# The order of branch groups and mixing steps, and which weight chunks live in one-time places

## The chip, the cores and the metric

One core of one Trainium2 chip runs the whole kernel. The metric is device time in microseconds (us). TensorE is called PE, VectorE DVE, ScalarE ACT and SyncE SP, as in the profile.

## The reference, cut to what matters

One encoder layer on 256 tokens of width 1024, in float32:

```
h      = rmsnorm(x);  proj = h @ w_in + b_in            # q, k, v, xr, yr, gates
merged = g_attn * (attn @ w_attn_o) + g_rec * (rec @ w_lru_o)
x      = x + merged @ w_out
h      = rmsnorm(x);  logits = h @ w_router + b_router  # top 4 of 32 experts
gu     = xb @ w_gu[e] + b_gu[e]                         # per expert, 1024 -> 2048
act    = clamp(g) * sigmoid(1.702 g) * (clamp(u) + 1)
y     += gate * (act @ w_down[e] + b_down[e])           # 1024 -> 1024
out    = rmsnorm(x + y)
```

The 32 experts hold 32 x 12.6 MB = 403 MB of weights, read once each from HBM.

## The kernel before

**Two halves.** The first half computes the token mixer. Its weights come as 15 "pre" chunks, each 128 x 4096 float32 (2 MB), that are split into a high and a low part; a product is three matmul passes over the parts. The second half walks the experts in order, 64 gathered tokens at a time; a step (one expert) uses six chunks of 2 MB, four of gate and up weights (`gate_up`, j = 0 to 3) and two of down weights of the expert before (`down`, j = 4 and 5). Step 0 has no down part, so expert chunks are numbered k = 0 to 3 for step 0 and then six to a step. PE uses the chunks in the order of k.

**Places.** Expert chunks live in a ring of eight 2 MB places: slots 0 to 6 (6 is `LOWS`) and slot 7, the tile `wide`. `SLOT_ORDER` says in which order the ring is walked. Two more chunks, named in `EXTRA`, go once into memory that the first half no longer needs: `late` takes the first, `pbuf` and `xr_flat` the two halves of the second. These one-time places are not refilled. `RING_CHUNKS` lists the chunks that use the ring; the one at index i goes to place `SLOT_ORDER[i % 8]` and its load waits until the chunk at index i - 8 has been used (`chunk_used`).

**Who issues.** SP issues all loads in one program order, each behind its wait. The first loads into a ring place wait for the first half to let go of it (`FREED`): slots 4 and 5 for six branch groups, slots 0 and 1 for `mixed_ps` 1 (mixing steps 0 to 3 done), `LOWS` for all eight branch groups, slots 2 and 3 for `mixed_ps` 2 (all mixing done). Half of `EXTRA[1]` and half of the chunk for `wide` are loaded some 30 us earlier, as memory allows. SP's program is written out for the first steps; a loop takes over after that.

**The work around the change.** `branches(g)`, g = 0 to 7, is one group of 128 output columns of the two branch products on PE (36 matmuls in two halves of a PSUM bank); banks 4 and 5 alternate. For g of 2 and more it first waits for `merged_ok` g - 1, which is the merge of group g - 2, the last user of its bank. On DVE the loop over g waits for the group (`branch_ps`), merges it with the gates in five instructions (L847, L849, L851, and the high and low parts, L621 and L624) and raises `merged_ok`; between groups it makes the low parts of pre chunks 12, 13 and 14 (`split_low`, L624). `mix(c)`, c = 0 to 3, multiplies merged block c with the first half of `w_out` into banks 0 to 3 (12 matmuls); `mix_end(n)` does blocks 4 to 7. Behind it come the second norm, the router and the first gather, and then step 0 of the experts.

Of the kernel before, what the change touches and what calls it, by code (L numbers as in the profile page):

```python
# [23 lines left out]
KD = D // P  # L24
# [15 lines left out]
SLOTS = 8  # L40
PAIRS = 3
PRE = 15
PER = 6
UNROLL = 4
# [11 lines left out]
def encoder_layer(nc, x, consts, squares, rows, pre, w_lru, w_gu, w_down, b_down, out):  # L56
# [5 lines left out]
    with ctx:  # L62
# [16 lines left out]
        LOWS = 2 * PAIRS  # L79
# [139 lines left out]
        dn_chunk = w_down.rearrange("e (p j r) n -> e j p (r n)", j=2, r=4)  # L219


        SLOT_ORDER = [4, 5, 0, 1, LOWS, SLOTS - 1, 2, 3]
        EARLIER = [5, 0, 5, 0, 4, 0, 1, 1]
        FREED = {4: [(branch_ps, 6)], 0: [(mixed_ps, 1)], LOWS: [(branch_ps, KD)], 2: [(mixed_ps, 2)]}

        EXTRA = (6, 11)
        RING_CHUNKS = [k for k in range(PER * UNROLL) if k not in EXTRA]

        def chunk_no(n, j):

# [41 lines left out]
        def expert_src(e, j):  # L272
            c = gu_chunk[e, j] if j < 4 else dn_chunk[e, j - 4]
            return c if isinstance(e, int) else c.rearrange("o p n -> (o p) n")


        @block.sync
        def _(sp):
            for t in range(T):
                sp.dma_start(x_sb[:, t, :], x[t * P:(t + 1) * P, :]).then_inc(x_in, 16)  # L280
            def expert_load(k):

                n, j = step_of(k)
                i = RING_CHUNKS.index(k)
                s = SLOT_ORDER[i % SLOTS]
                if i >= SLOTS:
                    n0, j0 = step_of(RING_CHUNKS[i - SLOTS])
                    sp.wait_ge(chunk_used[j0], n0 + 1 if j0 < 4 else n0 + AHEAD)
                else:
                    for freed in FREED.get(s, ()):  # L290
                        sp.wait_ge(*freed)
                sp.dma_start(slot(s), expert_src(n if j < 4 else n - 1, j)).then_inc(slot_full[s], 16)

            def half_load(dst, k, r, full):
                n, j = step_of(k)
                sp.dma_start(dst, expert_src(n, j)[:, r * 2048:(r + 1) * 2048]).then_inc(full, 16)

            for c in range(PRE):
                if c == 13:
                    sp.wait_ge(group_done, 32)  # L300
                    sp.wait_ge(gate_ps, 32)
                elif c == 14:
                    sp.wait_ge(pv_ps, NQ)
                    half_load(extra_rows(1, 0), EXTRA[1], 0, extra_full[1])
                    half_load(wide[:, 0:2048], 5, 0, slot_full[SLOTS - 1])
                    sp.wait_ge(branch_ps, 3)
                elif c >= PAIRS:
                    sp.wait_ge(*CONSUMED[c - PAIRS])
                sp.dma_start(whole(c), pre[c, :, 0:WIDTH[c]]).then_inc(slot_full[PLACE[c]], 16)
                if c == 1:  # L310
                    sp.dma_start(pbuf[:, 0:QKV + NH * HD], rows[0:1, 0:QKV + NH * HD].to_broadcast([P, QKV + NH * HD])
                                 ).then_inc(bias_in, 16)
                    o = QKV + NH * HD
                    sp.dma_start(brt[:, :], rows[0:1, o:o + NE].to_broadcast([P, NE])).then_inc(bias_in, 16)
                if c == 2:
                    sp.dma_start(cst[:, C_COS:], consts[:, C_COS:]).then_inc(tables_in, 16)
                    sp.dma_start(ring[LOWS][:, KD * TOK:], w_lru[0]).then_inc(lruw_in, 16)
                if c == 6:
                    sp.wait_ge(gate_ps, 16)
                    sp.dma_start(ring[LOWS][:, KD * TOK:], w_lru[1]).then_inc(lruw_in, 16)  # L320
            for k in range(5):
                expert_load(k)
            half_load(wide[:, 2048:], 5, 1, slot_full[SLOTS - 1])
            n, j = step_of(EXTRA[0])
            sp.dma_start(late[:, :], expert_src(n, j)).then_inc(extra_full[0], 16)
            sp.wait_ge(merged_ok, KD)
            half_load(extra_rows(1, 1), EXTRA[1], 1, extra_full[1])
            for k in RING_CHUNKS[6:-2]:
                expert_load(k)
            sp.wait_ge(passes_ok, 1)  # L330
            n_pass = sp.value_load(passes[0:1, 0:1], min_val=NE, max_val=NE * ROUNDS)

            def loop_load(n, i, place, j, e):
                s = SLOT_ORDER[(PER * i - 2 + place - len(EXTRA)) % SLOTS]
                n0, j0 = divmod(place - SLOTS, PER)
                sp.wait_ge(chunk_used[j0], sp.snap(n + (i + n0 + (1 if j0 < 4 else AHEAD))))
                src = expert_src(e, j) if isinstance(e, int) else expert_src(bass.ds(e, 1), j)
                sp.dma_start(slot(s), src).then_inc(slot_full[s], 16)

            with sp.Fori(UNROLL, n_pass, UNROLL) as n:  # L340
                for i in range(UNROLL):
                    e = sp.snap(sp.to_reg((n + i) & (NE - 1)), min_val=0, max_val=NE - 1)
                    e_before = sp.snap(sp.to_reg((n + i - 1) & (NE - 1)), min_val=0, max_val=NE - 1)
                    for j in range(PER):
                        loop_load(n, i, j, j, e if j < 4 else e_before)
            loop_load(n_pass, 0, 0, 4, NE - 1)
            sp.wait_ge(chunk_used[LAST_AFTER[1]], sp.snap(n_pass + LAST_AFTER[0]))
            for r in range(4):
                sp.dma_start(slot(LAST_SLOT)[:, r * D:(r + 1) * D],
                             expert_src(NE - 1, 5)[:, r * D:(r + 1) * D]).then_inc(last_in[r], 16)  # L350
            for n in range(2 * T):
                t, cols = n // 2, slice((n % 2) * BANK, (n % 2 + 1) * BANK)
                sp.wait_ge(fin_ok, n + 1)
                sp.dma_start(out[t * P:(t + 1) * P, cols], x_sb[:, t, cols]).then_inc(out_done_dma, 16)
            sp.wait_ge(out_done_dma, 16 * 2 * T)
# [224 lines left out]
        def _(dve):  # L580
# [263 lines left out]
            for g in range(KD):  # L844
                o = (g % 2) * TOK
                dve.wait_ge(branch_ps, g + 1)
                nc.vector.scalar_tensor_tensor(out=m_a[:, o:o + TOK], in0=gA[:, g, :], scalar=1.0,  # L847
                                               in1=half(4 + g % 2, 0), op0=ALU.add, op1=ALU.mult)
                link(nc.vector.scalar_tensor_tensor(out=m_r[:, o:o + TOK], in0=gR[:, g, :], scalar=1.0,  # L849
                                                    in1=half(4 + g % 2, 1), op0=ALU.add, op1=ALU.mult))  # L850
                link(nc.vector.tensor_tensor(merged[:, g, :], m_a[:, o:o + TOK], m_r[:, o:o + TOK], ALU.add))  # L851
                link(high_part(merged_hi[:, g, :], merged[:, g, :]))
                low_part(merged_lo[:, g, :], merged[:, g, :], merged_hi[:, g, :]).then_inc(merged_ok, 1)
                if g == 1:
                    split_low(12)
                if g == 2:
                    split_low(13)
                if g == 4:
                    split_low(14)

            dve.wait_ge(merged_ok, KD)
# [164 lines left out]
        def _(pe):  # L1026
# [149 lines left out]
            def branches(g):  # L1176
                first = 12 * g
                if g == 0:
                    pe.wait_ge(rec_split, 1)
                    pe.wait_ge(group_read, 32)  # L1180
                for i, c in enumerate(BR_CHUNK):
                    if first <= BLOCKS * i < first + 12:
                        chunk_in(c)
                if g >= 2:
                    pe.wait_ge(merged_ok, g - 1)
                w = [[b[:, q % BLOCKS, :] for b in w_br[q // BLOCKS]] for q in range(first, first + 12)]
                product(half(4 + g % 2, 1), [(w[k], (rec_hi[:, k, :], rec_lo[:, k, :])) for k in range(KD)])
                if g == 0:
                    pe.wait_ge(attn_split, 1)
                product(half(4 + g % 2, 0), [(w[KD + k], (attn_hi[:, k, :], attn_lo[:, k, :])) for k in range(4)]  # L1190
                        ).then_inc(branch_ps, 1)
# [8 lines left out]
            def mix(c):  # L1200
                if c == 0:
                    chunk_in(MIX_CHUNK[0])
                pe.wait_ge(merged_ok, c + 1)
                for n in range(2 * T):
                    ins = mix_bank(n, c)
                if c == 3:
                    ins.then_inc(mixed_ps, 1)
# [10 lines left out]
            for g in range(5):  # L1218
                branches(g)
            mix(0)  # L1220
            mix(1)
            branches(5)
            mix(2)
            mix(3)
            branches(6)
            branches(7)
            def second_transposes(t):
                pe.wait_ge(x2_ok, 2 * t + 2)
                if t == 1:
# [257 lines left out]
```

## Time and profile before

| | before |
|---|---|
| median of 3 runs | 1167.56 us (1165.97 to 1172.44) |
| profiled execution | 1171.78 us, of which span 1170.0 us |
| PE busy | 1086.2 us (93%) |
| DVE, ACT busy | 383.3 us (33%), 234.1 us (20%) |
| HBM read | 438.46 MB |
| mean granted TensorE clock | 0.993 |

The span runs from the first to the last instruction. The time of a run is a little longer than its span. Times inside the execution are counted from the start of the span. A busy PE is not PE at its peak, since matmuls overlap and their ends are modelled.

### The profile page before, as it was taken

Reading aid. Unit: us, or ns where it says so; the run is one execution under the profiler, and the core shown is the slowest. Engines: PE = TensorE matmul, PEld = TensorE weight load, DVE = VectorE, ACT = ScalarE, POOL = GpSimd, SP = SyncE. Lnnn points to the kernel's source line nnn. Section 1 sums busy time; section 2 is a strip of 40 time slices with the busy share of each in tenths; the row PEclk is TensorE's granted clock in tenths of the full one; section 3 lists DMA queues with packets and bytes.
Section 4 is the critical chain, followed back from the end, with each engine's and each line's share of the span. In section 5 each row is a group of like instructions: output and inputs, shape, how many; then the busy total and the mean of one; then the engine's idle time right before and its main releaser. Section 6 shows DMA issues by size and latency. Waiting matters only on the chain.

```text
span 1170.0 us, 13209 instructions
## 1 busy us (share of the span) xinstructions
PE 1086.2 (93%) x5391; PEld 507.2 (43%) x5391; DVE 383.3 (33%) x671; ACT 234.1 (20%) x371; POOL 0.2 (0%) x4
## 2 busy tenths in 40 slices
PE   6998999999999999999898989898989999999997
PEld 5997889833333333333233323332333333333332
DVE  6995699442322222221212121212121212212122
ACT  4387863111111111110101010101010101011112
POOL 0000000000000000000000000000000000000000
PEclk9998999999999999999999999999999999999999
DMA  8442326997999999999999999999999999999995
GB/s 342 179 182 96 121 89 272 390 428 308 401 430 425 429 427 428 428 427 429 429 429 427 429 429 429 429 427 429 427 429 429 429 427 430 427 429 430 428 429 239
DMA packets 32619, 439.90 MB, mean 376 GB/s; under 512 B 3760, under 2 KB 3888, under 8 KB 5712
## 3 DMA queue, kind: packets, MB, share of 16 engines
q1 hardware_dynamic: 32112, 438.53, 89.2%
q10 hardware_dynamic: 480, 0.99, 0.2%
q8 instruction: 20, 0.33, 0.1%
q14 instruction: 7, 0.06, 0.0%
HBM read 438.46 MB, written 1.05 MB: 376 GB/s over the span
## 4 chain that ended last, share of the span: by engine, by line
PE 59%; DMA 36%; DVE 2%; ACT 1%; issue 1%; SPq 0%; DVEq 0%
DMA slot<-in_w_gu_dram 29%; PE ps L1332 24%; PE ps L1034 12%; PE ps L1341 9%; DMA slot<-in_w_down_dram 6%; PE ps L1304 4%; PE ps L1285 3%; PE ps L1075 1%; PE ps L1089 1%; PE ps L1299 1%; PE ps L1386 1%; DMA slot<-in_pre_dram 1%; PE ps L1132 1%; PE ps L1263 1%; PE ps L1153 1%
## 5 line engine op out<-in xcount | busy, mean ns | idle before, releaser
L1332 PE MATMUL ps<-slot,lru 128*64 128x512 f32 x896 | 203.3, 596 | 25.7 <-DMA slot<-in_w_gu_dram 25.3
L1332 PE MATMUL ps<-slot,qT 128*64 128x512 f32 x880 | 200.2, 596 | 15.8 <-DMA slot<-in_w_gu_dram 14.2
L1341 PE MATMUL ps<-slot,lru 128*64 128x512 f32 x880 | 199.9, 596 | 15.3 <-DMA slot<-in_w_down_dram 14.9
L1332 PEld LDWEIGHTS ps<-slot,lru 128*64 128x64 f32 x896 | 63.0, 137 | 152.1 <-issue 113.1
L1332 PEld LDWEIGHTS ps<-slot,qT 128*64 128x64 f32 x880 | 62.6, 136 | 146.3 <-issue 131.8
L1341 PEld LDWEIGHTS ps<-slot,lru 128*64 128x64 f32 x880 | 61.1, 137 | 133.6 <-issue 114.3
L555 ACT ACTIVATE lru<-ps 128x512 f32<-128x512 f32 x32 | 19.1, 597 | 420.4 <-PE ps L1332 420.4
L990 DVE TENSOR_TENSOR lru<-ps,cst 128x1024 f32<-128x1024 f32 x32 | 39.2, 1225 | 142.9 <-PE ps L1386 142.9
L967 DVE TENSOR_SCALAR lru<-sq,x_sb,small 128x64 f32<-128x64 f32 x66 | 17.7, 311 | 189.4 <-PE ps L1285 189.4
L1034 PE MATMUL ps<-wide_r,slot_r 128*128 128x256 f32 x492 | 67.6, 290 | 0.0
L1034 PEld LDWEIGHTS ps<-wide_r,slot_r 128*128 128x128 f32 x492 | 62.9, 196 | 4.5 <-issue 4.4
L1304 PE MATMUL ps<-lru 128*128 128x512 f32 x136 | 63.9, 593 | 0.9 <-DVE lru L1014 0.9
L984 DVE COPY lru<-ps 128x512 f32<-128x512 f32 x32 | 22.1, 692 | 128.1 <-PE ps L1332 128.1
L1285 PE MATMUL ps<-hn,lru 128*64 128x512 f32 x264 | 62.9, 593 | 0.9 <-DVE lru L904 0.9
L624 DVE TENSOR_TENSOR slot_r<-slot,slot_r 128x4096 fp32r<-128x4096 f32 (+1 forms) x14 | 59.7, 4269 | 2.6 <-ACT slot_r L383 2.5
L557 ACT ACTIVATE lru<-lru 128x512 f32<-128x512 f32 x32 | 20.2, 630 | 199.7 <-DVE lru L994 199.7
L541 ACT ACTIVATE qT<-ps 128x512 f32<-128x512 f32 x33 | 19.7, 597 | 160.8 <-PE ps L1285 160.8
L934 DVE TENSOR_TENSOR qT<-ps,cst 128x512 f32<-128x512 f32 x16 | 11.1, 692 | 116.8 <-PE ps L1299 116.8
L383 ACT ACTIVATE slot_r<-slot 128x2048 fp32r<-128x2048 f32 (+1 forms) x24 | 43.1, 1836 | 22.2 <-DMA slot<-in_pre_dram 22.2
L548 ACT ACTIVATE lru<-ps 64x512 f32<-64x512 f32 x63 | 37.2, 591 | 39.8 <-PE ps L1341 39.0
L1386 PEld LDWEIGHTS ps<-sq,lru 128*128 128x128 f32 x256 | 30.8, 192 | 26.8 <-issue 25.1
L934 DVE TENSOR_TENSOR lru<-ps,cst 128x512 f32<-128x512 f32 x17 | 11.8, 692 | 88.3 <-PE ps L1299 88.3
(212 smaller groups left out, 914.1 us busy)
## 6 DMA issues: line engine op xcount, KB each, us to landing
slot<-in_w_gu_dram SPq DMA_DIRECT2D x111, 2048.0 KB, 34.9
slot<-in_w_down_dram SPq DMA_DIRECT2D x55, 2048.0 KB, 34.2
slot<-in_pre_dram SPq DMA_DIRECT2D x14, 2048.0 KB, 8.2
wide<-in_w_gu_dram SPq DMA_DIRECT2D x14, 2048.0 KB, 35.0
wide<-in_w_down_dram SPq DMA_DIRECT2D x8, 2048.0 KB, 33.2
slot<-in_w_lru_dram SPq DMA_DIRECT2D x2, 1024.0 KB, 13.8
wide<-in_w_gu_dram SPq DMA_DIRECT2D x2, 1024.0 KB, 17.3
late<-in_w_gu_dram SPq DMA_DIRECT2D x1, 2048.0 KB, 21.3
```

Source lines behind the costliest of these rows:

```text
L383: nc.scalar.activation(high(c)[:, i * w:(i + 1) * w], whole(c)[:, i * w:(i + 1) * w], ACT.Copy).then_inc(split_hi, 1)
L548: nc.scalar.activation(pair_out[i // 2 % 2][rs, side * BANK:(side + 1) * BANK], ps[64 * side:64 * side + 64, bank, :], ACT.Copy).then_inc( ...
L624: return nc.vector.tensor_tensor(dst, whole, hi.bitcast(f32), ALU.subtract)
L934: nc.vector.tensor_tensor(xgT[i % 2].rearrange("p (h k) n -> p k h n", h=2), ps[:, 7, :].rearrange("p (k h n) -> p k h n", k=KD // 2, h=2) ...
L984: nc.vector.tensor_copy(gu_sb[:, 0:BANK], ps[:, 4, :]).then_inc(gu_v, 1)
L990: nc.vector.tensor_tensor(gub.rearrange("p (j n) -> p j n", j=16), ps[:, 4:6, :].rearrange("p b (j n) -> p (b j) n", n=CAP), bias.unsqueez ...
L1034: ins = nc.tensor.matmul(dst, st[a], mv[b], start=start and q == 0 and k == 0, stop=stop and q == 2 and k == len(sides) - 1)
L1285: ins = nc.tensor.matmul(ps[64 * h:64 * h + 64, 7, :], sel_next[:, t, :], x2[:, t, h * BANK:(h + 1) * BANK], start=(t == 0), stop=(t == T ...
L1304: return nc.tensor.matmul(ps[:, n, :], sgT[pair][:, n // 2, :], pair_out[pair][:, (n % 2) * BANK:(n % 2 + 1) * BANK], start=False, stop=last)
L1332: ins = nc.tensor.matmul(ps[64 * side:64 * side + 64, 4 + b, :], xgT[i % 2][:, k, :], rows[r][:, o:o + BANK], start=(k == 0), stop=(k == K ...
L1341: ins = nc.tensor.matmul(ps[64 * side:64 * side + 64, bank, :], actT[(i - 1) % 2][:, k, :], w[:, r, side * BANK:(side + 1) * BANK], start= ...
L1386: ins = nc.tensor.transpose(ps[:, 4 + j // 4, j % 4 * P:(j % 4 + 1) * P], gu_sb[:, j::KD], ident)
```

## The change

PE does branch groups 5, 6 and 7 straight after mixing step 0, and mixing steps 1, 2 and 3 after them. The ring is walked in the order 4, 5, `LOWS`, `wide`, 0, 1, 2, 3, so that chunks 0 and 1 stay in slots 4 and 5, chunks 2 and 3 go to `LOWS` and `wide`, and chunks 4 to 7 to slots 0 to 3. The one-time places hold chunks 18 and 19 instead of 6 and 11. SP issues chunks 0, 1, 2, the rest of 3, chunk 18, then 4 and 5, the rest of 19, and then 6, 7, 8 and so on. SP's written-out program covers eight steps instead of four. The low part of pre chunk 14 is made behind the merge of group 5 instead of group 4.

```diff
-        SLOT_ORDER = [4, 5, 0, 1, LOWS, SLOTS - 1, 2, 3]
+        SLOT_ORDER = [4, 5, LOWS, SLOTS - 1, 0, 1, 2, 3]
...
-        EXTRA = (6, 11)
-        RING_CHUNKS = [k for k in range(PER * UNROLL) if k not in EXTRA]
+        EXTRA = (18, 19)
+        SP_UNROLL = 2 * UNROLL
+        RING_CHUNKS = [k for k in range(PER * SP_UNROLL) if k not in EXTRA]
...
-                    half_load(wide[:, 0:2048], 5, 0, slot_full[SLOTS - 1])
+                    half_load(wide[:, 0:2048], 3, 0, slot_full[SLOTS - 1])
...
-            for k in range(5):
+            for k in range(3):
                 expert_load(k)
-            half_load(wide[:, 2048:], 5, 1, slot_full[SLOTS - 1])
+            half_load(wide[:, 2048:], 3, 1, slot_full[SLOTS - 1])
             n, j = step_of(EXTRA[0])
             sp.dma_start(late[:, :], expert_src(n, j)).then_inc(extra_full[0], 16)
+            for k in (4, 5):
+                expert_load(k)
             sp.wait_ge(merged_ok, KD)
...
-            with sp.Fori(UNROLL, n_pass, UNROLL) as n:
+            with sp.Fori(SP_UNROLL, n_pass, UNROLL) as n:
...
-                if g == 4:
+                if g == 5:
                     split_low(14)
...
             mix(0)
-            mix(1)
-            branches(5)
-            mix(2)
-            mix(3)
-            branches(6)
-            branches(7)
+            for g in range(5, KD):
+                branches(g)
+            for c in range(1, 4):
+                mix(c)
```

## Rows read from the trace of the kernel before

**Rows 1.** Page, the span in 40 slices: DMA engines' busy tenths, and GB/s.
```profile
DMA  8442326997999999999999999999999999999995
GB/s 342 179 182 96 121 89 272 390 428 308 401 430 425 429 427 428 428 427 429 429 429 427 429 429 429 429 427 429 427 429 429 429 427 430 427 429 430 428 429 239
```

**Rows 2.** Stretches: window, length, each engine's busy time, PE clock, DMA share, GB/s.
```profile
200.00:206.00 6.00, 6.00 (x45) 5.69 (x44) 4.99 (x3) 0.27 (x1) 0.00 (x0) 1.00 0.00 0
...
285.00:290.00 5.00, 5.00 (x22) 1.49 (x22) 0.54 (x1) 0.54 (x1) 0.00 (x0) 1.00 0.00 0
...
289.00:292.00 3.00, 3.00 (x16) 1.00 (x14) 0.69 (x1) 0.60 (x1) 0.00 (x0) 1.00 0.59 169
...
310.00:320.00 10.00, 10.00 (x52) 3.89 (x52) 3.10 (x5) 0.63 (x2) 0.00 (x0) 1.00 0.95 357
345.50:500.00 154.50, 154.50 (x714) 55.41 (x715) 35.38 (x69) 17.80 (x30) 0.00 (x0) 1.00 1.01 428
```

**Rows 3.** Chain that ended last, in order of time: start, length, what.
```profile
1116.70 35.42 DMA slot<-in_w_down_dram
```

**Rows 4.** PE in order of time, branch groups and mixing.
```profile
195.46 5.63 PE L1034 MATMUL ps<-slot_r,lru_r 128*128 128x512 f32 x24
200.93 0.64 PE L1034 MATMUL ps<-lru_r,slot_r 128*128 128x256 f32 x4
...
205.24 5.63 PE L1034 MATMUL ps<-slot_r,lru_r 128*128 128x512 f32 x24
...
219.34 8.67 PE L1034 MATMUL ps<-slot_r,lru_r 128*128 128x512 f32 x36
```

**Rows 5.** DVE in order of time: the ends of merges 3 and 4, and the split.
```profile
196.77 0.43 DVE L624 TENSOR_TENSOR lru_r<-lru,lru_r 128x256 fp32r<-128x256 f32 x1
...
198.68 0.42 DVE L624 TENSOR_TENSOR lru_r<-lru,lru_r 128x256 fp32r<-128x256 f32 x1
200.30 4.42 DVE L624 TENSOR_TENSOR slot_r<-slot,slot_r 128x4096 fp32r<-128x4096 f32 x1 [1.20 <-ACT slot_r L383]
...
221.12 0.42 DVE L624 TENSOR_TENSOR lru_r<-lru,lru_r 128x256 fp32r<-128x256 f32 x1
```

**Rows 6.** SP's issues in order of time.
```profile
205.43 14.43 SPq L292 DMA_DIRECT2D slot<-in_w_gu_dram  x5
...
289.45 11.86 SPq L292 DMA_DIRECT2D slot<-in_w_gu_dram  x4
309.56 4.50 SPq L292 DMA_DIRECT2D slot<-in_w_down_dram  x2
...
345.56 0.34 SPq L338 DMA_DIRECT2D slot<-in_w_gu_dram  x1
```

**Rows 7.** Chain that ended last, 240 to 350 us: expert chunks on PE.
```profile
245.61 3.69 PE ps L1332 x16
...
279.94 3.58 PE ps L1332 x16
...
285.83 3.58 PE ps L1332 x16
...
326.94 3.43 PE ps L1332 x16
...
341.93 3.43 PE ps L1341 x16
```

**Rows 8.** DMA queues of SP (q1) and ACT (q10), 200 to 345.5 us: packets, MB, share.
```profile
q1 hardware_dynamic: 3847, 54.12, 89.9%
q10 hardware_dynamic: 192, 0.66, 1.1%
```

**Rows 9.** One issue each, at 289.45 and at 345.56 us: size, us to landing.
```profile
slot<-in_w_gu_dram SPq DMA_DIRECT2D x1, 2048.0 KB, 7.2
...
slot<-in_w_gu_dram SPq DMA_DIRECT2D x1, 2048.0 KB, 13.6
```

## The prediction

> **What bounds the kernel now.** I read the page's slices first, then the stretches, then the chain. From slice 11 to slice 38 the DMA engines move 425 to 430 GB/s without a break [rows 1], 428 over 345.5 to 500 us [rows 2], while PE is near fully busy too. The chain of waits decides between the two: its last long piece is a load that lands at 1152.1 us, 35.4 us after its issue [rows 3], and the 17.9 us behind it are the last products, the final norm and the store. So the end is the moment when SP's queue has moved its last byte, plus 17.9 us. Each chunk of 2.097 MB costs 4.90 us at 428 GB/s. The bytes do not change, so the whole change is worth what it takes out of the queue's idle time ahead of the unbroken stretch. A late hole costs whatever an earlier start had won: what counts is how far behind its issues the queue is at the last moment at which PE's releases, and not the queue, set the pace.
>
> The slices show two places with idle queue: 200 to 206 us moves nothing and 285 to 290 us moves nothing [rows 2]; slices 9 and 10 have 308 and 401 GB/s [rows 1]. The first hole is the wait for six branch groups: the first expert loads are issued at 205.43 [rows 6]. The second is a full ring: from step 0's start at 245.61 [rows 7] on, a place comes free only when PE has used a chunk.
>
> **The branch order and the first issues.** One branch group takes 4.31 us (200.93 to 205.24) and one mixing step 2.74 (half of the 5.47 from 195.46 to 200.93) [rows 4]. Groups 0 to 4 end at 195.46. Group 5 ends at 205.24 now, behind two mixing steps [rows 4]; afterwards behind one, at 202.5. So chunks 0 and 1 go out 2.7 us earlier. Groups 6 and 7 follow, to 206.8 and 211.1, where chunk 2, half of 3 and chunk 18 go out; mixing 1 to 3 ends at 219.4 (as group 7 does now, at 219.34 [rows 4]), where 4, 5 and half of 19 go; 6 and 7 stay behind all mixing, near 231.5. None of these waits leaves the queue dry: 0 and 1 take 9.8 us to 213.9, the next 2.5 chunks 12.3 us to 226.2, the next 2.5 to 238.5. No chunk comes too late for PE: 6 and 7, the last of these, are there by 250, and 6 is used at 279.94 [rows 7].
>
> Does PE stall in the new order? Group 5 starts at 198.2 and needs merge 3, which ends at 197.20 (196.77 + 0.43); group 6 starts at 202.5 and needs merge 4, over at 199.10 [rows 5]; group 7 starts at 206.8 and needs merge 5, which starts when group 5 ends and takes 2.0 us (1.9 lie between the ends of merges 3 and 4 [rows 5]), so 204.6. Slack 1.0, 3.4 and 2.2 us. The low part of pre chunk 14, 4.42 us [rows 5], now falls behind merge 5 (204.6 to 209.0), delays merge 6 by 2.2 us to 211.0, and merge 7 ends at 213.4; PE wants that split and those merges only from 219.4 on. If that cover were gone it would cost up to 4.4 us. Queued behind it on DVE are the memsets ahead of the second residual, which gain. A stall goes away: mixing step 7 now waits for merge 7, which ends at 221.54 [rows 5], and the 36 matmuls from 219.34 take 8.67 us [rows 4] where 1.5 times 5.47 plus the last matmul's tail of 0.16 makes 8.37. I take 0.2 us for it (bounds 0 and 0.3). PE is otherwise unbroken to the router, so step 0 and all releases come 0.2 us earlier.
>
> **The one-time places.** Filling all ten places ends some 3 us earlier, near 249.7: 204.1 (202.7 plus the 1.4 us of a restart, below) plus nine chunks' worth (44.1) plus 0.66 MB that ACT's queue adds [rows 8] (1.5). Chunk 8 can only be issued when chunk 0 has been used, at 249.3 (245.61 + 3.69 [rows 7]). So the early start by itself ends as waiting, and is worth nothing. What counts is the next part. Now chunk 6 is in `late`: its use at 279.9 to 283.5 frees nothing that is loaded again, and the next issue comes when chunk 7 is done, 285.83 + 3.58 [rows 7], issued at 289.45 [rows 6]. That is the hole at 285 to 290. Afterwards chunk 6 is in slot 2 and its use at 283.5 issues chunk 14. Chunk 11's use frees a place as well, one chunk of 3.43 us ahead of chunk 12's, whose release is the issue at 309.56 [rows 6]: at 306.1.
>
> A restart of an idle queue costs this: issue at 289.45, and by 292 it had moved 169 GB/s x 3 us = 0.51 MB, 1.2 us' worth of the 2.55 [rows 2, 6], so 1.4 us are lost. From 289.45 on the two orders compare simply. Before: chunks 16 to 27, twelve of them, 290.85 + 4 x 4.90 = 310.45 for 16 to 19, then chunk 20 from 309.56 + 1.4 = 310.96, a gap of 0.5, and 8 x 4.90 from there: 350.2. The trace's own count: by 345.5 SP had issued 27 chunks' worth since 205.43 (56.62 MB) and its queue had moved 54.12 MB [rows 8]; 2.50 MB are left, 5.8 us, so chunk 28, issued at 345.56 [rows 6], really starts at 351.4. The 1.2 us between the two counts are bandwidth lost with a short queue (357 GB/s in 310 to 320 us [rows 2]).
>
> After: the issue at 289.45 is chunk 15, and 15, 16, 17 and 20 to 27 are eleven chunks: 290.85 + 11 x 4.90 = 344.8, with 1.2 us lost as before 346.0. All of them are issued in time (27 goes when 17 is used, 326.94 + 3.43 [rows 7], and its turn is 339.9). But now the uses of 18 and 19, from 332 to 342 us, free nothing. Chunk 28 goes to the place of chunk 20 in both orders, and that one is used up at 345.4 (341.93 + 3.43 [rows 7]). So 28 is issued at 345.56 and starts 1.4 later, at 347.0: a new hole of 1.0 us, and **the gain is capped by PE's release at 351.4 - 347.0 = 4.4 us**, however much the earlier holes shrink. Behind the new hole the queue is short again for three or four chunks, with issues 3.5 to 5 us apart. The row for 310 to 320, the same situation, lost 71 of 428 GB/s over 10 us, 1.7 us, of which 0.5 are the gap itself. I subtract the other 1.1 us: 3.3.
>
> SP's longer written-out part has the same issues with constant addresses; issues take 0.33 us in both forms and 27 chunks were issued with waits between them, so I cost it at nothing. If SP's issue came late by 1 us at the wrong place it would cost that once.
>
> **Sum.** 4.4 - 1.1 + 0.2 = 3.5 us less. The profiled span goes from 1170.0 to 1166.5, and its own time from 1171.8 to 1168.3; that execution was 4.2 us above the median, so the median goes from 1167.56 to 1164.1.
>
> A count by landings gives another size. Chunk 28 lands 13.6 us after its issue, at 359.2; a chunk into an idle queue lands after 7.2 [rows 9], so at 352.8: 6.4 us less, 6.6 with the stall. I go by bytes, since at 359.2 the other engines had already moved part of chunk 29. The Trainium skill (DMA: Bandwidth & Descriptors, Queues, rings and completion order) says that a copy is split over up to 16 rings and that each engine consumes its own in order, so a chunk counts as landed only with its slowest engine; that speaks for bytes. The same page (Anatomy of one DMA) gives 2.0 us plus the bytes at 436 GB/s, an estimate of 6.8 us for a chunk alone where the row has 7.2; by it the landing count would say 6.8 us less.
>
> **Rivals.**
> - Landings are the right measure and the sag does not come: 1167.56 - 6.6 = 1161.0. For it: the 7.2 us row. Against: the byte count.
> - Every hole is won back, the second one (from 285 at the latest [rows 2] to 290.85, 5.9 us), the gap of 0.5 and the 2.7 us at the start, with the new hole hidden: 1167.6 - 5.9 - 0.5 - 2.7 - 0.2 = 1158.3. It needs chunk 28 to find a queue still busy, against the release time of chunk 20.
> - No gain: the queue loses more than 4 us between 291 and 347 because it stays short longer, or the new hole at 345 to 347 comes with a second one behind chunk 29 or 31. The win is given back: 1167.6. Against: the same situation at 310 to 320 us lost 1.7 us in all [rows 2].
> - Slower: PE stalls between the three adjacent branch groups. If each of groups 5, 6 and 7 had to wait for the merge just before it, that is 3 x 2.0 + the split's 4.4 = 10.4 us later for step 0 and for every release, one for one: 1164.1 + 10.4 = 1174.5. It decides from a DVE delay of 1.0 us at group 5 on, and reaches +0.5% at 9.3 us of stall. Against: the wait is for the group two before.
>
> **Chances.** The forecast (a gain of 1.5 to 5.8 us) 0.59; landings 0.17; all holes 0.06; no gain 0.11; slower 0.07. A measurement of this kernel tells about 0.5%, 5.8 us, from no change. Faster by more: 0.17 + 0.06 = 0.23; within: 0.59 + 0.11 = 0.70; slower: 0.07. The range goes down to the landing count less 1.5 us of spread of a median of these runs, 1159.5, and up to no gain plus as much, 1169.1; outside are all holes and the slower rival.
>
> **What would show it.** First expert issue at 202.7; group 5, 6, 7 back to back without a gap on PE; step 0 at 245.4. No stretch without bytes at 285 to 290; instead one of about 1 us (0 to 2) at 345 to 347, with chunk 28 landing 7 to 9 us after its issue. From 200 to 345.5 us SP's queue has moved some 56.4 MB instead of 54.12. The first PE wait for a load comes later than now. Wrong it would be if the queue were still a chunk behind at 345.5, if step 0 moved by more than 0.5 us, or if the rate of the unbroken stretch differed from 428 GB/s: 1 GB/s there is 1.9 us.

## The result and the profile after

The changed kernel takes 1163.76 us in the median of 20 runs (1161.31 to 1167.10) against 1168.90 us for the kernel before in as many: a ratio of 0.996, with a 95% interval of 0.995 to 0.997 (3.5 to 5.8 us). The gain is 5.1 us; 3.5 were forecast. Two smaller comparisons further down gave 3.5 and 4.5 us. The time itself, forecast at 1164.1 us, came out that near only because the median of before rose by 1.3 us from three runs to twenty.

The page's slices of the changed kernel, to set beside [rows 1]:

```profile
DMA  8543146998999999999999999999999999999996
GB/s 351 186 171 145 73 160 278 418 400 333 429 397 425 431 425 429 428 428 429 428 429 428 430 428 427 430 428 428 430 428 428 429 428 430 428 427 429 429 428 248
```

From slice 12 on the rate is about the same 428 GB/s as before. The stretches of the changed kernel (window, length, busy time of each engine, PE clock, DMA share, GB/s), to set beside [rows 2]:

```profile
190.00:196.00 6.00, 6.00 (x43) 5.60 (x42) 2.95 (x8) 3.72 (x2) 0.00 (x0) 1.00 0.00 0
200.00:206.00 6.00, 6.00 (x49) 5.87 (x48) 5.51 (x8) 0.00 (x0) 0.00 (x0) 1.00 1.02 437
285.00:290.00 5.00, 5.00 (x27) 2.02 (x24) 0.69 (x1) 0.60 (x1) 0.00 (x0) 1.00 0.91 334
341.50:344.50 3.00, 3.00 (x18) 1.60 (x18) 1.58 (x3) 0.00 (x0) 0.00 (x0) 1.00 0.64 202
```

The empty stretch ahead of the first loads is still there; it only lies at another place, since this execution reaches the branch groups some 6 us earlier (below). It lasts 8.0 us, from the last packet of the pre chunks to the first of the expert loads, against 10.3 before. The empty stretch at 285 to 290 us is gone, and there is a thin one at 341.5 to 344.5 us that before did not have. SP's issues of the changed kernel in order of time, as in [rows 6]:

```profile
196.75 8.97 SPq L293 DMA_DIRECT2D slot<-in_w_gu_dram  x3
...
279.92 6.22 SPq L293 DMA_DIRECT2D slot<-in_w_down_dram  x2
...
321.65 5.48 SPq L293 DMA_DIRECT2D slot<-in_w_down_dram  x2
341.79 0.33 SPq L293 DMA_DIRECT2D slot<-in_w_gu_dram  x1
```

Before, 11.6 us passed from one issue to the next (277.88 to 289.45) while chunk 6 was used; now chunk 14 goes out there, at 279.92, and a pause of 15.0 us (326.80 to 341.79) stands where chunks 18 and 19 are used. Chunk 27 is the issue at 326.80, the second of the row of 321.65, and chunk 28 the one at 341.79. SP's queue (q1) from the first expert load up to there, with its packets, MB and share, and the landing of that chunk (size, us to landing), as in [rows 8, 9]:

```profile
q1 hardware_dynamic: 4027, 56.58, 94.7%
```

```profile
slot<-in_w_gu_dram SPq DMA_DIRECT2D x1, 2048.0 KB, 7.4
```

56.58 of the 56.62 MB issued had moved: the queue was as good as empty, where before it was 2.50 MB behind ("behind" is what has been issued and has not moved yet). At chunk 27's issue it was 4.08 MB behind, 6.17 with that chunk; the pause of 15.0 us is long enough to move 6.42 at 428 GB/s, so it only just ran dry.

**How to compare two executions.** The profiled spans differ by 8.8 us (1170.0 and 1161.2), more than the medians. Two rows tell why. The long piece of the chain that starts with the first branch group:

```profile
167.81 53.91 PE ps L1037 x372
```

It starts at 167.81; the same group started at 173.76 in the kernel before, with nothing changed ahead of it. That 5.95 us belongs to the executions: in later profiles of the changed kernel it starts at 173.66 and 173.48. It goes with TensorE's granted clock (full speed is 2.4 GHz, the other level 1.2). From 100 to 120 us the kernel before has a mean of 0.74 (the third number from the end of its row below). In the changed kernel it is 1.00 there, and in the later profile that starts at 173.66 it is 0.74 again. Over the fourteen profiles the group starts at 167.7 to 169.2 us where this mean is 1.00, at 169.4 where it is 0.91, at 170.9 where it is 0.83 and at 172.1 to 173.8 where it is 0.74.

```profile
100.00:120.00 20.00, 16.85 (x78) 13.72 (x77) 10.25 (x16) 13.08 (x28) 0.00 (x0) 0.74 0.27 98
```

Then, the chain of the changed kernel around step 0:

```profile
234.72 1.98 PE ps L1286 x4
...
240.34 3.65 PE ps L1333 x16
...
263.70 5.35 PE ps L1333 x16
```

The four matmuls at L1286 take 1.98 us and the 16 of chunk 4 take 5.35; in other executions of the same kernel they take 1.08 and 3.65. The granted clock of 265 to 270 us has a mean of 0.76 here and is 1.00 again at 290 to 295. Before it fell, PE was busy for 4.68 of the 7 us from 257 to 264. The later profile that starts at 173.66 has the same 4.68 us in that place (262 to 269), and the clock stays at 1.00 there: the same work can meet the lower level in one execution and not in another. The distance from the first branch group to step 0 has two values 1.0 us apart for each branch order (71.50 and 72.53 us in the new one, 71.85 and 72.86 in the old; near waits, below, stand apart), and the one from step 0 to chunk 28's issue two values 1.5 us apart, 99.9 and 101.5. The longer of these last came in five of the ten profiles of the new branch order and in none of the four of the old. Each run also has its mean granted clock, and there are more runs than profiles: it was 0.996 or more in 20 of 107 runs of kernels with the new order (without near waits) and in 43 of 126 with the old one, and among the runs of the kernel before those with such a clock were some 3 us shorter. So the new order may lose a little on average to a lower clock; no comparison below is fine enough to show it. What is steady is the rest: **from chunk 28's issue to the end** it is 1170.0 - 345.56 = 824.4 us before and 1161.2 - 341.79 = 819.4 us after, 5.0 less. So 5.0 us are gained behind chunk 28's issue, and the rest of the 8.8 is the 5.95 less the 2.2 that this execution lost between the first branch group and that issue. The table below uses the steady part.

### The profile page after: what moved, and what is told of

It is laid out like the page before. It is cut to its first block, busy times and chain, and to the rows that moved or that the text cites. A ratio compares the mean times of both kernels' runs of the same rounds, so it can differ in the third digit from the quotient of the medians.

```text
span 1161.2 us, 13145 instructions
## 1 busy us (share of the span) xinstructions
PE 1081.6 (93%) x5391; PEld 502.8 (43%) x5391; DVE 382.9 (33%) x671; ACT 234.2 (20%) x371; POOL 0.2 (0%) x4
## 4 chain that ended last, share of the span: by engine, by line
PE 61%; DMA 33%; DVE 4%; ACT 1%; issue 1%; SPq 0%; DVEq 0%
DMA slot<-in_w_gu_dram 27%; PE ps L1333 25%; PE ps L1037 12%; PE ps L1342 10%; DMA slot<-in_w_down_dram 6%; PE ps L1305 4%; PE ps L1286 3%; PE ps L1300 1%; PE ps L1387 1%; DVE slot_r L627 1%; PE ps L1092 1%; PE ps L1135 1%; PE ps L1264 1%; PE ps L1156 1%; PE ps L1365 0%
## 5 line engine op out<-in xcount | busy, mean ns | idle before, releaser
L970 DVE TENSOR_SCALAR lru<-sq,x_sb,small 128x64 f32<-128x64 f32 x66 | 17.7, 312 | 188.1 <-PE ps L1286 188.1
L1286 PE MATMUL ps<-hn,lru 128*64 128x512 f32 x264 | 63.7, 600 | 0.9 <-DVE lru L907 0.9
```

The lines of the kernel that those rows point to most:

```text
L1286: ins = nc.tensor.matmul(ps[64 * h:64 * h + 64, 7, :], sel_next[:, t, :], x2[:, t, h * BANK:(h + 1) * BANK], start=(t == 0), stop=(t == T ...
```

## The experiments

Three columns for each kernel, all from its profile: MB that SP's queue had moved since the first expert load, at chunk 28's issue and 50 us after it, and us from that issue to the end of the span. The last column is the ratio of the runs to those of the kernel before.

| kernel | at 28 | 50 us on | to the end | ratio (95%) |
|---|---|---|---|---|
| before | 54.12 | 75.45 | 824.4 | 1 |
| order alone | 54.13 | 75.45 | 824.3 | 1.0011 (0.9997 to 1.0024) |
| longer SP program | 53.99 | 75.35 | 824.7 | 1.0001 (0.9987 to 1.0016) |
| one-time 12, 13 | 55.22 | 76.55 | 822.1 | 0.998 (0.9967 to 0.9992) |
| changed kernel | 56.58 | 77.33 | 819.4 | 0.996 (0.995 to 0.997) |
| again, e3 | 56.56 | 77.38 | 819.4 | 0.9977 (0.9958 to 0.9995) |
| again, e12 | 56.56 | 77.25 | 819.8 | 0.9968 (0.9954 to 0.9981) |
| chunks alone | 56.59 | 77.37 | 819.4 | 0.9962 (0.9948 to 0.9977) |
| near waits | 56.59 | 77.40 | 819.6 | 1.0008 (0.9997 to 1.0018) |
| longer PE program | 56.59 | 77.38 | 819.6 | 0.997 (0.9954 to 0.9987) |
| one-time 30, 31 | 56.82 | 78.22 | 818.7 | 0.9957 (0.9942 to 0.9971) |
| again, e11 | 56.85 | 78.20 | 818.6 | 0.9966 (0.9954 to 0.9978) |
| 30, 31, old order | 56.81 | 78.20 | 818.8 | 0.9963 (0.995 to 0.9976) |
| one-time 42, 43 | 56.84 | 78.19 | 818.6 | 0.9959 (0.9946 to 0.9973) |

**Chunks alone.** The kernel before, with

```diff
-        EXTRA = (6, 11)
-        RING_CHUNKS = [k for k in range(PER * UNROLL) if k not in EXTRA]
+        EXTRA = (18, 19)
+        SP_UNROLL = 2 * UNROLL
+        RING_CHUNKS = [k for k in range(PER * SP_UNROLL) if k not in EXTRA]
...
-            with sp.Fori(UNROLL, n_pass, UNROLL) as n:
+            with sp.Fori(SP_UNROLL, n_pass, UNROLL) as n:
```

> The kernel before with the one-time places given to chunks 18 and 19 (and SP's written-out program of eight steps that this needs); branch order and order of places as before. Theory A, the pace of PE's releases: the last moment at which PE's releases set the pace is the issue of chunk 28, and that moment does not depend on when the first loads started. So nearly the whole gain of the change comes with this part: 4.7 us less than before (4.0 to 5.5), no idle queue at 40 to 45 us after step 0's start, and a new hole of about 1 us some 100 us after it. Theory B, the earlier first loads: 2.7 us of the gain belong to them, so this kernel gains 2.4 us at most.

Measured: 1163.48 us against 1168.16, 4.7 less, and 819.4 us from chunk 28's issue. Its stretches (columns as before):

```profile
285.00:290.00 5.00, 5.00 (x26) 1.82 (x23) 0.69 (x1) 0.60 (x1) 0.00 (x0) 1.00 0.97 357
341.50:344.50 3.00, 3.00 (x20) 1.50 (x18) 1.24 (x2) 0.00 (x0) 0.00 (x0) 1.00 0.63 180
```

The old hole is closed and the new one is there, with the old branch order. Theory A holds; the 2.4 us of theory B lie just outside the interval (2.7 to 6.1 us less), and the profile's 5.0 us are twice that.

**Order alone.** The changed kernel, with

```diff
-        EXTRA = (18, 19)
-        SP_UNROLL = 2 * UNROLL
+        EXTRA = (6, 11)
+        SP_UNROLL = UNROLL
```

> The changed kernel with the one-time places given back to chunks 6 and 11; the new branch order and the new order of places stay. Theory A: the first loads go out 2.7 us earlier against the branch groups, the places are full earlier and the queue then stands idle that much longer; only the 0.2 us of a removed stall ahead of step 0 remain, so 0.2 us less than before (0 to 0.5), and the 5 us of idle queue ahead of chunk 16's issue are still there. Theory B: 2.7 us less.

Measured: 1169.65 against 1168.16 us; the interval reaches from 0.4 us less to 2.8 us more, so not the 2.7 us of theory B. The first loads did go out early (199.86, which is 28.9 us behind the first branch group at 170.92, against 31.7 before), and the stretch where they end up waiting is this kernel's

```profile
280.00:285.00 5.00, 5.00 (x22) 1.79 (x18) 0.69 (x1) 0.00 (x0) 0.00 (x0) 1.00 0.74 318
285.00:290.00 5.00, 5.00 (x24) 1.64 (x25) 0.69 (x1) 0.60 (x1) 0.00 (x0) 1.00 0.11 23
```

the old hole. At chunk 28's issue it had moved 54.13 MB, against 54.12 before. The median lies 1.5 us above before, where theory A had it 0.2 below; whether that is noise or the clock named above is not shown.

**The changed kernel again**, unedited, as yardstick.

> The changed kernel once more, on the same chip as the other three, as their yardstick. 5 us less than the kernel before (3.5 to 6).

Measured: 1164.64 us, 3.5 less. The interval, 0.6 to 4.9 us, is wide: one of the ten runs took 1171.47 us at a mean granted clock of 0.944.

**One-time places for 30 and 31.** The changed kernel, with

```diff
-        EXTRA = (18, 19)
+        EXTRA = (30, 31)
...
-            for n in range(1, UNROLL):
-                step(n, n)
+            for n in range(1, SP_UNROLL):
+                step(n, n % UNROLL)
...
-            with pe.Fori(UNROLL, n_pass, UNROLL) as n:
+            with pe.Fori(SP_UNROLL, n_pass, UNROLL) as n:
```

> The changed kernel with the one-time places given to chunks 30 and 31 (step 5), and PE's written-out program of eight steps that this needs. Theory A: when the uses of 30 and 31 free nothing, the queue is more than two chunks behind, so the new hole of 1 to 2 us ahead of chunk 28 disappears and no other comes. The queue's last wait for PE is then the one near 45 us after step 0's start. 2.1 us less than the changed kernel by the count of chunks of 4.90 us, up to 3.2 if the loss of bandwidth behind the hole goes too. A rival, that the hole is only a symptom and the time is set elsewhere: the same as the changed kernel, within 0.5 us.

Measured: 1162.24 us against 1168.16 before and 1164.64 of the changed kernel. The hole is gone; this kernel's stretch around chunk 28's issue (342.83):

```profile
340.00:345.00 5.00, 5.00 (x28) 2.17 (x26) 1.18 (x2) 0.01 (x1) 0.00 (x0) 1.00 1.02 433
```

The uses of 30 and 31 make the same pause of 15.0 us, from 380.39 to 395.39, but the queue was 8.90 MB behind when it began (with the chunk just issued) and still 2.50 behind when it ended. 50 us on from chunk 28's issue it had moved 78.22 MB, 0.88 MB or 2.1 us' worth more than the changed kernel, as counted ahead. But to the end it was only 0.75 us faster. One more quantity tells where the rest went: the bytes still to come when the load lands for which PE waits last. That load is the last whole chunk; behind it the final one comes as four loads of 0.52 MB, 2.10 in all. From that landing on SP's queue moved, in the changed kernel, then in this one, then in the kernel before (queue, packets, MB, share, 12 us each):

```profile
q1 hardware_dynamic: 398, 1.41, 29.4%
```

```profile
q1 hardware_dynamic: 281, 0.98, 20.4%
```

```profile
q1 hardware_dynamic: 340, 1.20, 25.2%
```

So part of the four later loads had moved before the chunk ahead of them had landed: 0.69 MB in the changed kernel, 1.12 in this one. The end hangs on the landing of that chunk (it comes 17.7 us behind it in every profile but the first, which has 17.9), and 0.43 MB less still out at it is 1.0 us taken back. Moved bytes plus those still out account for every row: the kernel before has 75.45 + 1.20 = 76.65, the changed one 77.33 + 1.41 = 78.74, and 2.09 MB at 428 GB/s are 4.9 us of the 5.0; with 30 and 31 it is 79.20, 6.0 of 5.8 us.

**One-time places for 12 and 13.** The changed kernel, with

```diff
-        EXTRA = (18, 19)
+        EXTRA = (12, 13)
```

> The changed kernel with the one-time places given to chunks 12 and 13 (step 2). Theory A: their uses, some 60 us after step 0's start, free nothing while the queue is only one to two chunks behind, so the queue runs dry there, and PE's releases set the pace once more up to chunk 27; by the count of chunks of 4.90 us the queue is 1.4 us further back than in the changed kernel. 1.4 us more than the changed kernel (0.7 to 2.5), 3 to 4 us less than the kernel before. A rival, that only chunk 6's place mattered, since the 5 us hole stood there: the same as the changed kernel.

Measured: 1165.69 against 1168.76 us. After the issue that waits for the use of chunk 11 there is no other from 303.71 to 314.75, and this kernel's stretches there and at chunk 28's issue are

```profile
310.00:315.00 5.00, 5.00 (x25) 1.66 (x22) 0.69 (x1) 0.60 (x1) 0.00 (x0) 1.00 0.59 249
315.00:320.00 5.00, 5.00 (x28) 2.10 (x28) 3.37 (x5) 1.20 (x2) 0.00 (x0) 1.00 0.85 321
340.00:345.00 5.00, 5.00 (x28) 2.13 (x26) 1.18 (x2) 0.17 (x1) 0.00 (x0) 1.00 0.97 374
```

The first hole is there because the queue was 1.87 MB behind at 303.71, 3.97 with the chunk issued there, and the pause of 11.0 us is long enough to move 4.7. 50 us after chunk 28's issue it is 0.79 MB, 1.8 us, behind the changed kernel, and 2.7 us to the end; the other 0.9 us are again the last landing (0.99 MB still out against 1.41), which the expected 0.7 to 2.5 us had no term for. The rival, that only chunk 6 mattered, would have it at 819.4.

**Near waits.** The changed kernel, with

```diff
-                pe.wait_ge(merged_ok, g - 1)
+                pe.wait_ge(merged_ok, g - 1 if g < 5 else g)
```

> The changed kernel with branch groups 5, 6 and 7 each made to wait for the merge just before it instead of the one before that: the slower rival of the prediction, made real. PE should stand idle 0.9 + 2.0 + 6.4 us ahead of groups 5, 6 and 7 (the last one with the split of pre chunk 14), and step 0 starts 9.3 us later against the first branch group. Theory A, PE's releases set the pace until chunk 28: the end comes later by the same amount, 9.3 us (8 to 10.4), and the stretch from chunk 28's issue to the end is unchanged at 819.4 us. A rival, that the slack of the queue hides part of it since all first loads are waiting in their places: less than 5 us.

PE's rows at the starts of groups 5, 6 and 7, with the idle time ahead of them in brackets:

```profile
194.46 0.71 PE L1037 MATMUL ps<-lru_r,slot_r 128*128 128x256 f32 x4 [0.88 <-DVE lru_r L627]
...
201.09 1.22 PE L1037 MATMUL ps<-lru_r,late_r 128*128 128x256 f32 x8 [2.09 <-DVE lru_r L627]
...
207.75 1.22 PE L1037 MATMUL ps<-lru_r,late_r 128*128 128x256 f32 x8 [2.09 <-DVE lru_r L627]
```

5.1 us of stall, not 9.3: I had counted the split of pre chunk 14 as exposed, but it runs on DVE from 200.95 to 205.4 beside group 6 itself. Each group also takes longer when PE starts it from idle: from the start of group 5 to that of group 6 it is 6.6 us, and without the 2.09 of idle time that is 4.5, where a group took 4.31 on end. So step 0 starts 78.3 us behind the first branch group, 5.8 more than the changed kernel in an execution that is as slow around step 0 (72.53). From step 0 to chunk 28's issue it is 100.06 us, as in the shorter executions of the others, and from there to the end 819.6. So nothing of the delay is hidden by the queue, as theory A said, though my figure for the delay was wrong. The time was 1169.0 us, 4.4 to 5.2 above the medians of the changed kernel (1163.76 to 1164.64 in its three timings), which takes the whole gain of the change back. The expected figure for the rival (less than 5 us) fits this time no worse; only the two stretches of the profile tell the theories apart.

**Longer SP program.** The kernel before, with SP's written-out program of eight steps.

```diff
+        SP_UNROLL = 2 * UNROLL
...
-            with sp.Fori(UNROLL, n_pass, UNROLL) as n:
+            with sp.Fori(SP_UNROLL, n_pass, UNROLL) as n:
```

> The kernel before with SP's written-out program of eight steps instead of four, and nothing else. Costed at nothing: the same time as before within 0.1%, and 824.4 us from chunk 28's issue to the end, as in the kernel before. If constant addresses made the issues faster or the longer program were fetched late, this kernel would differ.

1168.89 against 1168.76 us: nothing, as costed.

**Longer PE program.** The changed kernel, with PE's part of the diff of 30 and 31 alone.

> The changed kernel with PE's written-out program of eight steps instead of four, and nothing else: the part that the kernel with one-time chunks 30 and 31 had besides. The same as the changed kernel within 0.1%, 819.4 us from chunk 28's issue to the end. If it is faster by itself, the step from 18 and 19 to 30 and 31 is worth less than it seemed.

1164.60 us, 819.6 from chunk 28's issue: nothing by itself, so what 30 and 31 gain is theirs.

**30 and 31 in the old order.** The kernel before, with the diff of chunks alone, 30 and 31 in `EXTRA`, and the longer PE program.

> The kernel before (old branch order, old order of places) with the one-time places given to chunks 30 and 31 and the longer written-out programs of SP and PE. Theory A: the branch order is worth nothing here too, so this is the kernel with 30 and 31 in the new order over again: 78.2 MB moved by 50 us after chunk 28's issue, 818.7 us from that issue to the end, 5 to 6 us less than before in the median. Theory B, that the earlier first loads count once the late hole is gone: 2 to 2.7 us more than with the new order.

78.20 MB and 818.8 us, 1163.08 in the median: theory A again. Even without the late hole the early first loads count for nothing. No stretch is empty behind step 0 here, but at chunk 15's issue, some 44 to 45 us behind step 0, this kernel and the one with the new order had moved the same 33.29 MB and were 0.26 behind: there the queue still waits for PE.

**One-time places for 42 and 43**, **30 and 31 again**, and **the changed kernel a second time**, the first with `EXTRA = (42, 43)` in the diff of 30 and 31.

> The changed kernel with the one-time places given to chunks 42 and 43 (step 7), the last that the written-out programs reach. Theory A: once no hole follows the one near 45 us after step 0's start, it does not matter how much later the one-time places are used: the same bytes moved by 50 us after chunk 28's issue as with 30 and 31 (78.2 MB) and the same time within 1 us. If the last loads' unequal landing over the 16 DMA engines is what takes back half of the 2 us there, it may come out up to 1 us either way.

> The kernel with one-time chunks 30 and 31 once more, beside the changed kernel on one chip. Its profile had 0.75 us less than the changed kernel between chunk 28's issue and the end, where the count of bytes said 2.1. 0.7 to 2 us less than the changed kernel; the stretch of 818.7 us should come back if it belongs to the kernel and not to the execution.

> The changed kernel a second time, as yardstick for the other three: 3.5 to 5.5 us less than the kernel before, and 819.4 us from chunk 28's issue to the end.

Measured: 1162.46, 1163.52 and 1164.17 us. How late the places are used makes no difference once no hole follows (78.19 MB, 818.6 us); the 818.6 us of 30 and 31 came back, so they belong to the kernel. 30 and 31 are 0.65 us below the changed kernel here (0.7 to 2 were expected) and were 2.4 below it in the first comparison; the profiles say 0.7 to 1.2. The intervals of their ratios overlap that of the changed kernel, so it is seen in the profiles and not resolved by the runs.

## Why the prediction was right, step by step

- **What bounds the kernel.** Right. The rate of the long stretch is 428 GB/s before (345.5 to 500 us) and 427 after (345 to 500), and from 50 us behind chunk 28's issue to the last landing that PE waits for it is 428.1 in both (323.9 MB in 756.6 us, 321.8 MB in 751.7). The bytes moved at a fixed point, with those still out at that landing, give the stretch to the end to within 0.3 us in all fourteen profiles. This is a balance of bytes at one rate; what shows the cause is that moving the one-time places alone moves both.
- **First loads 2.7 us earlier.** Right in size (28.94 us after the first branch group, against 31.67) and right that they are worth nothing: the order alone had moved 54.13 MB by chunk 28's issue, before 54.12.
- **No stall between the branch groups, 0.2 us less to step 0.** Right. PE runs 372 matmuls on end where before it had 345 and a wait; of the two levels of the distance to step 0 each is 0.33 to 0.35 us lower, the term being 0.2 with a bound of 0.3, so the size was a little outside its bound.
- **Chunk 6's place closes the hole, and chunk 28's release caps the gain.** Right: no empty stretch at 285 to 290, the queue empty at chunk 28's issue, a thin stretch behind it. Before, 2.50 MB were left there; now 0.04. The release of chunk 20 is the cap: with 30 and 31 the hole is not there, and 2.1 us more are won in bytes.
- **The cap of 4.4 us.** 2.46 MB are 5.7 us; the restart and all that follows it cost 0.57 MB in the 50 us from the issue (20.76 MB against 21.33), 1.3 us. That leaves 4.4 us.
- **Minus 1.1 us for a sag behind the hole.** This is the term that was mis-sized: it is 0. The 1.3 us just named hold the restart and every loss behind it, and the restart alone had been put at 1.4. I had taken the whole loss of the stretch from 310 to 320 us, but for the gap of 0.5, as the price of a short queue. In that stretch the queue was down to 0.38 MB at chunk 20's issue, so it probably holds most of a restart as well; that split is argued, not measured.
- **What was not in the sum.** The last landing: 1.41 MB still out instead of 1.20 is 0.5 us on the side of the change. With it, 4.4 + 0.5 = 4.9 of the 5.0 us, and the 0.35 ahead of step 0 makes 5.3 for a measured 5.1. The other two comparisons gave 3.5 and 4.5, so the runs can't tell whether that 0.35 arrives; the terms behind chunk 28's issue are checked by the profiles. The sag and the last landing erred on the same side, so the forecast was 1.5 us short.
- **The rivals.** The count by landings (7.4 us instead of 13.6, 6.2 less) overstated it, as the byte count said: when chunk 28 landed before, at 359.15, SP's queue had moved 59.89 MB, 1.17 more than all chunks up to it. The estimate of 6.8 us for a chunk alone, from the Trainium skill (DMA: Bandwidth & Descriptors, Anatomy of one DMA), is given there for loads that GpSimd issues; here SP issues them, and they took 7.0 to 7.8. All holes won back: no, the new one is there. The slower rival was priced at 10.4 us; made real, it put step 0 back by 5.8 and cost 4.4 to 5.2 in the runs.
- **The check on the first PE wait.** Before, PE first waits for a load in the window of 500 to 540 us, now in that of 540 to 580.

Why a chunk at the end lands with 1.41 MB of later ones out in one arrangement and with 0.98 in another is open. It repeats between executions of one kernel (0.98 and 0.99 with 30 and 31; 1.41, 1.38 and 1.24 in the changed kernel), but no experiment changed it by itself.

## What to carry to other kernels

When a saturated queue sets the end, look for the last moment at which a consumer's release, not the queue, sets the pace; only what the queue has moved by then counts, and starting the first transfers earlier is worth nothing if they end up waiting for a full ring. A place that is filled once and not refilled leaves a gap where it is used: give it to a piece at whose use the queue has more left to move than the pause lasts. Here two such uses made a pause of 15.0 us, three chunks' worth: with 18 and 19 the queue had 6.17 MB left and just ran dry, with 30 and 31 it had 8.90 and did not. Moving the places from 6 and 11 to 18 and 19 gave 5 us, and 30 and 31 some 0.7 to 1.2 more in the profile. To compare two executions whose early parts differ by more than the change is worth, measure from a common event in the middle to the end.

## What the runs showed of the hardware

From chunk 28's issue to the end, executions of one kernel agreed within 0.5 us out of 819, while the start of their first branch group differed by up to 5.9 us (167.81 to 173.66). That difference goes with the granted clock: its mean from 100 to 120 us is 0.74 where the group starts at 172.1 or later, and 1.00 where it starts before 169.3. Later in the execution dips of the clock fall on different instructions: four L1286 matmuls take 1.08 or 1.98 us, the 16 of chunk 4 3.65 or 5.35. A 2 MB load into an idle queue landed after 7.0 to 7.8 us; behind a queue 2.5 MB long it took 13.6. Later loads of one queue move before an earlier one has landed: 1.17 MB of them at chunk 28's landing before, 0.69 to 1.12 MB at the last whole chunk's.
